# The second feed-forward stage of a transformer kernel, from plain products to block products with seven multiplications

## The reference, cut to what matters

```
mix = jnp.concatenate([y_pool, y_sb], axis=-1) @ w_out[i]
h = h + rms_norm_2(mix, g_mix_post[i])

m = rms_norm_2(h, g_mlp_pre[i]) @ w_up[i]
m = jnp.square(jax.nn.relu(m)) @ w_down[i]
h = h + rms_norm_2(m, g_mlp_post[i])
```

## Time and profile before

| | |
|---|---|
| median of 3 runs | 2649.5 us (2647.52 to 2650.82) |
| profiled execution, its own time | 2642.97 us |
| its span, first to last instruction | 2641.2 us |
| PE busy | 2422.6 us, 92% of the span |
| DVE / ACT / POOL busy | 1435.7 / 897.7 / 1034.2 us |
| mean granted TensorE clock | 0.952 of full speed |
| second feed-forward at full pace | from 1819.02 us on, to 2493.71 us |

### The profile page before, as it was taken

One profiled execution on the slowest core, in us unless ns is written; L12 is line 12 of the kernel. 1 busy time (PEld: TensorE's weight loads), 2 busy tenths in 40 slices (PEclk: granted clock), 3 DMA queues, 4 the chain that ended last, 5 costly groups with the idle time before them and its releaser, 6 DMA issues.

```text
span 2641.2 us, 28134 instructions
## 1 busy us (share of the span) xinstructions
PE 2422.6 (92%) x10656; PEld 1886.1 (71%) x10656; DVE 1435.7 (54%) x1534; ACT 897.7 (34%) x1339; POOL 1034.2 (39%) x628
## 2 busy tenths in 40 slices
PE   8988877989999999999788887968999999999978
PEld 6855645868888878877555554656888888888757
DVE  7788863586656666477355456457222222222566
ACT  4255554244444432221365466213001100110231
POOL 1000000468878778774111020244333334444353
PEclk9999988989999999999899896989999999999989
DMA  3211101314344368832000000211111111111102
GB/s 126 56 33 30 32 17 64 120 41 151 128 175 160 136 257 323 343 140 80 16 25 16 9 8 1 104 40 32 48 48 48 48 48 48 48 48 48 56 32 88
DMA packets 64540, 215.86 MB, mean 82 GB/s; under 512 B 20465, under 2 KB 20465, under 8 KB 57905
## 3 DMA queue, kind: packets, MB, share of 16 engines
q1 hardware_dynamic: 63776, 210.03, 22.1%
q10 hardware_dynamic: 656, 4.41, 0.4%
HBM read 161.24 MB, written 53.35 MB: 81 GB/s over the span
## 4 chain that ended last, share of the span: by engine, by line
PE 69%; issue 11%; DVE 10%; ACT 5%; POOL 4%; DMA 1%; SPq 0%; POOLq 0%; DVEq 0%; ACTq 0%
PE ps L702 39%; PE ps L971 21%; PE ps L1173 3%; DVE conv_out L1915 1%; PE ps L1105 1%; POOL weight_hi L578 1%; POOL weight_lo L580 1%; ACT sb_e L1694 1%; DMA weight_raw<-w_out 1%; ACT sb_e L1692 1%; POOL turn_weights L616 1%; POOL branch_out L661 1%; ACT sb_e L1696 1%; DVE sb_softplus_lo L2437 1%; PE ps L1148 1%
## 5 line engine op out<-in xcount | busy, mean ns | idle before, releaser
L578 POOL TENSOR_TENSOR weight_hi<-weight_raw,zero_col 128x1024 fp32r<-128x1024 f32 (+1 forms) x106 | 205.2, 1936 | 1371.7 <-PE ps L702 1111.0
L971 PE MATMUL ps<-operand,turn_weights 128*128 128x512 f32 x1848 | 427.0, 393 | 11.9 <-DVE operand L2112 7.2
L702 PE MATMUL ps<-input_lo,weight_hi 128*128 128x512 f32 x1328 | 419.2, 397 | 16.7 <-DVE gate_lo L2548 14.9
L702 PE MATMUL ps<-input_hi,weight_hi 128*128 128x512 f32 x1200 | 387.2, 404 | 50.5 <-DVE input_lo L1873 32.1
L971 PEld LDWEIGHTS ps<-operand,turn_weights 128*128 128x128 f32 x1848 | 350.2, 190 | 89.0 <-issue 13.6
L702 PE MATMUL ps<-input_hi,weight_lo 128*128 128x512 f32 x1200 | 374.5, 394 | 0.0
L702 PEld LDWEIGHTS ps<-input_lo,weight_hi 128*128 128x128 f32 x1328 | 254.5, 192 | 74.3 <-ACT input_lo L1279 11.4
L702 PEld LDWEIGHTS ps<-input_hi,weight_hi 128*128 128x128 f32 x1200 | 224.5, 192 | 112.0 <-issue 52.9
L616 POOL TENSOR_TENSOR turn_weights<-turn_raw,turn_weights 128x512 fp32r<-128x512 f32 (+1 forms) x170 | 234.5, 1390 | 93.7 <-ACT turn_weights L1279 92.8
L580 POOL TENSOR_TENSOR weight_lo<-weight_raw,weight_hi 128x1024 fp32r<-128x1024 f32 (+1 forms) x106 | 262.7, 2478 | 8.3
L702 PEld LDWEIGHTS ps<-input_hi,weight_lo 128*128 128x128 f32 x1200 | 228.5, 190 | 48.9
(11 more groups left out here) (299 smaller groups left out, 3689.4 us busy)
## 6 DMA issues: line engine op xcount, KB each, us to landing
hidden_operand<-hidden_kept SPq DMA_DIRECT2D x35, 1024.0 KB, 8.5
hidden_kept<-hidden_parts SPq DMA_DIRECT2D x22, 1024.0 KB, 11.2
turn_raw<-w_ff SPq DMA_DIRECT2D x40, 512.0 KB, 3.9
hidden_kept<-hidden_parts SPq DMA_DIRECT2D x11, 1536.0 KB, 8.9
weight_raw<-w_mlp SPq DMA_DIRECT2D x32, 512.0 KB, 3.3
weight_raw<-w_mlpd SPq DMA_DIRECT2D x32, 512.0 KB, 3.3
turn_raw<-w_ffd SPq DMA_DIRECT2D x20, 512.0 KB, 4.3
weight_raw<-w_out SPq DMA_DIRECT2D x16, 512.0 KB, 3.3
```

Of the source, the lines that this page charges most:

```text
L578: pool_.tensor_tensor(WH[:, slot, 0:width], raw, ZERO[:].to_broadcast([P, width]), ALU.add).then_inc(s["w_hi"], 1)
L702: last = mm(PS[:, b + 2 * c + h, :], w[:, slot, k * n + P * c:k * n + P * (c + 1)], a[:, k, h * H2:(h + 1) * H2], start=(k == first and st ...
L971: ins = mm(PS[:, b, :], weights(p, w, k), tokens(p, a, k), start=(FRESH[p] and k == 0 and step == 0), stop=(k == n - 1 and step == 2), ski ...
```

## The change

The second feed-forward gets the same treatment as the first: an instance `FF_B` with 16 hidden turns and 16 output turns. What differs from `FF_A`: there is no gate, so one turn makes a whole pair, and seven parts are made and written out in every turn, not in every second one. The blocks stay in PSUM: relu with scale (DVE) and square (ACT) work in place, and the sums of blocks go to PSUM too. Of seven products, three (p = 0, 1, 2) are copied by ACT (`kept_term`) to be added to later ones. The squares for the norm ahead of the stage are summed by TensorE (`add_to_mean`, a matmul with the mean matrix for each row) and no longer by DVE. POOL no longer scales rows; DVE does it.

```diff
+FF_B = Ff(1, FF_A.end, FF2 // P // 2, tuple((2 * g, 2) for g in range(NG2)), (0, 1, 2, 3, 4, 5, 6),
+          (32, 40, 48, 56, 64, 72, 80, 88, 128, 136), (0, 3, 5, 1, 4, 2, 6), 1)
...
@@ SP
+            turn_load(FF_B.t0)
+            turn_load(FF_B.t0 + 1)
+            for k in range(KD):
+                x_kept(FF_B, k)
+            stage_transfers(FF_B)
+            def stage_transfers(ff):
+                for t in range(ff.t0 + 2, ff.t2 + 2):
+                    turn_load(t)
...
+                    elif t >= ff.t0 + 3:
+                        parts_out(ff, t - 3 - ff.t0)
+                for p in range(N_PROD):
+                    parts_in(ff, 0, p)
...
@@ POOL
-            pool.wait_ge(s["scale_ready"], 4)
-            for k in range(1, KD):
-                pool_.tensor_tensor(MM[:, k, :], MM[:, k, :], RS[:], ALU.mult).then_inc(s["post_scaled"], 1)
-            splits(U_MLP + 2, U_PLEP - U_MLP - 2)
+            for t in range(FF_B.t0, FF_B.end):
+                turn_split(t)
...
@@ TensorE
+                if n == 0 and ff is FF_B:
+                    pe.wait_ge(s["scale_ready"], 4)
+                    for k in range(4):
+                        add_to_mean(k)
...
+                    elif ff is FF_B:
+                        if p in (0, 1, 3):
+                            pe.wait_ge(s["st_fl"], N_PROD * pairs_to(ff, n - 2))
...
+                    if p in (2, 4, 5):
+                        pe.wait_ge(s["st_mid"], 3 * (FF_A.n1 * ff.index + n) + {2: 1, 5: 2, 4: 3}[p])
                     elif p == 6:
                         pe.wait_ge(s["st_read"], read_at(t, 4))
...
-            with pe.Fori(1, NG2) as i:
-                ff_group(i, U_MLP, G, 1, 0)
+            for t in range(FF_B.t0, FF_B.t2):
+                hidden_turn(FF_B, t)
+            for t in range(FF_B.t2, FF_B.end):
+                output_turn(FF_B, t)
...
@@ ScalarE, one hidden turn
+                for q in range(3):
+                    block_hi(n - 1, q)
+                kept_term(t, 0)
+                turn_hi(t + 1, 0)
+                block_hi(n - 1, 3)
+                block_hi(n - 1, 4)
+                kept_term(t, 1)
+                turn_hi(t + 1, 1)
+                block_hi(n - 1, 5)
+                block_hi(n - 1, 6)
+                kept_term(t, 2)
+                turn_hi(t + 1, 2)
+                turn_hi(t + 1, 3)
+                squared(t, 0)
...
+            def block_hi(n, q):
+                act.wait_ge(s["st_sqd"], 6 * (n + 1))
+                act.wait_ge(s[f"st_sp{(0, 0, 0, 1, 1, 2, 2)[q]}"], 16 * pairs_to(FF_B, n - 1))
...
@@ VectorE, each row ahead of the stage
-                    dve.wait_ge(s["post_scaled"], k)
-                stt(X[:, k, :], MM[:, k, :], g("g_mix_post", k), X[:, k, :], ALU.mult, ALU.add)\
-                    .then_inc(s["post_x"], 1)
+                mark = chain(stt(MM[:, k, :], MM[:, k, :], g("g_mix_post", k), RS[:], ALU.mult, ALU.mult))
+                chain.wait(mark)
+                tt(X[:, k, :], X[:, k, :], MM[:, k, :], ALU.add).then_inc(s["post_x"], 1)
+                first_sums(FF_B, k, "g_mlp_pre")
+            other_operands(FF_B, "g_mlp_pre")
+            for j in range(4):
+                op_lo(FF_B, 6, j, raw_at(FF_B, 6, j))
             scale_from(5)
...
@@ VectorE, one hidden turn
+                total(3, 0, b0 + 1)
+                block(0, b0 + 1, lower)
+                total(4, 1, 6 + t % 2, "st_read")
+                dve.wait_ge(s["st_read"], read_at(t, 4))
+                block(1, 6 + t % 2, upper)
+                total(5, 2, b0 + 2)
+                block(2, b0 + 2, upper)
+                dve.wait_ge(s["st_prod"], prod(t, 6))
+                block(3, b0, lower)
...
+            for t in range(FF_B.t0, FF_B.t2):
+                if t > FF_B.t0:
+                    block_parts(t - FF_B.t0 - 1)
+                squared_terms(t)
```

More of the change, by code:

```diff
@@ L129, with __init__ @@
 class Ff:
-    def __init__(self, t0, n1, groups, place, ring):
-        self.t0, self.n1, self.groups, self.place, self.ring = t0, n1, groups, place, ring
+    def __init__(self, index, t0, n1, groups, place, ring, kept, reads):
+        self.index, self.t0, self.n1, self.groups, self.place, self.ring = index, t0, n1, groups, place, ring
+        self.kept, self.reads = kept, reads
         self.t2 = t0 + n1
@@ L1789, in _ @@
+            for t in range(FF_B.t2, FF_B.end - 1):
+                for p in range(N_PROD):
+                    turn_hi(t + 1, p)
+                    if t == FF_B.t2 + 2 and p > 3:
+                        last_hi(p - 4)
+                    elif t == FF_B.t2 + 3 and p < 4:
+                        last_hi(p + 3)
             act.wait_ge(s["ple_p_in"], 16)
@@ L2094, in _, with op_at, op_sum @@
             lower, upper = slice(0, H2), slice(H2, T)
[L2096 to L2099 removed]
+            def op_at(ff, p, part, j):
+                return FORM[ff.place[p]][:, part, j, :]
+            def op_sum(ff, p, j, out, x, gain, y, op):
                 if gain is None:
@@ L2265, in output_term @@
                 dve.wait_ge(s["st_read"], reads_to(t) + p)
-                last = p in (3, 4, 5, 6) and g_ == len(ff.groups) - 1
+                last = p in (3, 4, 5, 6) and g_ == len(ff.groups) - 1 and ff is FF_A
                 if g_ == 0 and p in (0, 1, 2, 6):
@@ new lines, in block_parts, with total, lo @@
+            def block_parts(n):
+                t = FF_B.t0 + n
+                b0, there, spare = 3 * (t % 2), PS[:, 6 + t % 2, :], PS[:, 7 - t % 2, :]
+                one, two, three = PS[:, b0 + 1, :], PS[:, b0 + 2, :], PS[:, b0, :]
+                done, low_ = 4 * (PAIRS_A + n), N_PROD * (PAIRS_A + n)
+                def total(i, out, x, y, op):
+                    tt(out, x, y, op).then_inc(s["st_ft"], 1)
+                    dve.wait_ge(s["st_ft"], done + i)
+                def lo(q, src):
+                    dve.wait_ge(s["st_fh"], low_ + q + 1)
+                    tt(STG[:, q, 1, :], src, STG[:, q, 0, :].bitcast(f32), ALU.subtract).then_inc(s["st_fl"], 1)
+                dve.wait_ge(s["st_sqd"], 6 * (n + 1))
+                if n:
+                    dve.wait_ge(s["st_fl"], low_)
+                total(1, spare, two, TB[:, lower], ALU.subtract)
+                total(2, two, TB[:, upper], two, ALU.subtract)
+                total(3, TA[:, upper], TB[:, upper], spare, ALU.subtract)
+                lo(0, one)
+                lo(1, three)
+                dve.wait_ge(s["st_fl"], low_ + 2)
+                total(4, three, three, TA[:, upper], ALU.subtract)
+                lo(2, there)
+                lo(3, spare)
+                lo(4, two)
+                lo(5, TA[:, upper])
+                lo(6, three)
@@ new lines, in _ @@
+            for t in range(FF_B.t0, FF_B.t2):
+                if t > FF_B.t0:
+                    block_parts(t - FF_B.t0 - 1)
+                squared_terms(t)
+            for t in range(FF_B.t2, FF_B.end):
+                for p in range(N_PROD):
+                    output_term(FF_B, t, p)
+                    if FF_B.group(t)[0] == 1:
+                        last_pair_of(FF_B, t, p)
+                    elif t == FF_B.end - 1 and p < 2:
+                        dve.wait_ge(s["ple_hi"], p + 1)
+                        tt(PPL[:, p, :], PPF[:, p, :], PPH[:, p, :].bitcast(f32), ALU.subtract)\
@@ L2532, in p_and_squares @@
                             .then_inc(s["ple_lo"], 1)
+                    elif t == FF_B.end - 1 and p < 6:
+                        add_square()
+            for k in range(4, KD):
                 add_square()
-                if m:
-                    add_square()
-            dve.wait_ge(s["bank_free"], (NG2 - 1) * (2 * G) + U_MLP)
-            dve.wait_ge(s["ff_acc"], (NG2 - 1) * 4)
-            ff_lo(NG2 - 1, U_MLP, G, 1, h0, MM, beside=p_and_squares)
-            add_square()
             scale_from(6)
+            dve.wait_ge(s["st_back"], 16 * 4)
```

610 lines of the change are left out of this document (330 added, 280 removed).

## The result

The changed kernel took 2604.0 us (median of four runs, 2598.8 to 2606.9), beside 2648.5 us for the kernel before, also of four runs (2646.0 to 2650.8): a ratio of 0.983, 95% interval 0.981 to 0.985, which is 44.5 us less. The forecast was 2603.5 us. The profiled execution took 2602.29 us with a span of 2600.5 us.

A forecast was written before the change was run, and what follows sets the result against it. Bound: TensorE's matmuls, and the seams between them. Stage end 2493.7 to 2445.1, 48.6 us less, 2.5 more at the tail: 46 less, 2597 profiled; plus 6.5 for the median, 2603.5 us, range 2592 to 2621.

The forecast's parts named there:

- The matmuls: Second feed-forward: 2688 matmuls instead of 3072 at 0.2268 us, 87.1 us less; hidden turns of 19.05 us, nothing charged.
- The seam ahead: Before the second feed-forward: DVE's instruction list is the bound, so product 6 of the first turn starts at 1847.7 us.
- (a): Last sum of squares ahead of the stage: 1.9 us less, scale ready at 1769.0 us instead of 1770.87.
- Rows: Seam ahead: DVE's work on the eight residual rows takes 49.7 us, the last row done at 1818.7 us.
- (c): Seam ahead: 24 DVE operations for the other tiles, 16.6 us uncontended; ACT's guess sets the middle, ending at 22.7 us.
- The restart: TensorE starting again at half clock at product 6 of the first turn: 1.6 us more until it is back up.
- The seam to the output turns: From hidden to output turns: the first operand's read follows the last writes, 1.5 us, bounds 0 and 3 us.
- The tail: Behind the stage, up to the mean: squares and adds one by one, and DVE running late, 2.5 us more.
- The stretched turns: Hidden turns: the 1.7 us to spare at product 2 used up, 1 us a turn, 16 us, 2619 us; chance 0.13.
- starved output turns: Output turns that also read the residual back: DMA too slow, up to 5 us, 2609 us; chance 0.07.
- The slower case: Hidden turns: high parts wait for the last pair's landing in the single buffer; 23 us a turn, 2663 us; chance 0.05.
- the fourth rival: DMA starving output turns: 17 MB in two turns, 43 us of 38 at 410 GB/s, up to 5 us; chance 0.07.

The follow-up runs named there:

- blocks_sbuf: Changed kernel with the squared blocks of every hidden turn written to SBUF, not PSUM; 2605.9 us, ratio 0.9851 to before.
- rows_ahead: Changed kernel with DVE adding residual row k+1 before it makes the operands of row k; 2590.6 us, ratio 0.9783 to before.
- guess_late: Changed kernel with ACT's first guess of the scale moved behind the high parts of operands 4 and 5; 2601.8 us.
- read_early_copy: read_early, with ACT's copy of the second turn's first kept term moved right behind the second block's squares; 2596.2 us.
- seam_read_first: Changed kernel with the output turns' first operand read issued ahead of the writes of the last but one pair's parts; 2597.4 us.
- parts_twice: Changed kernel with each portion of parts written to device memory twice, the next pair's high parts waiting for both writes; 2630.4 us.
- tail_even_first: Changed kernel with ACT squaring rows 4, 6, 5, 7 after the last output term, the first two one term earlier; 2594.2 us.
- together_late_read: Changed kernel with the edits of rows_ahead, guess_late, seam_read_first and tail_even_first; 2582.4 us, ratio 0.9748 to before.
- read_early: Changed kernel with the first turn's two sums that need no scale taken ahead of operand 6's low parts and the scale; 2603.4 us.

## Why the prediction was right, point by point

**The matmuls.** Predicted 2688 at 0.2268 us, a hidden turn of 19.05 us, nothing charged for the 16 turns. The 240 us window without a pause shows it, and blocks_sbuf shows why it was safe: 2.5 us more on DVE and 1.5 us more on POOL in each turn cost nothing there. The latency was counted well too: in the third turn ACT's copy of product 0 ended at 1879.24 us and product 2 was due at 1881.1, 1.8 us to spare where 1.7 was predicted. The 1050 ns that the prediction took for an operation with both sides in SBUF is a mean of fast and slow ones (shortest, median and longest in ns):

```profile
L2235 DVE TENSOR_TENSOR hidden_parts<-hidden_parts x26: 678/840/1777, 650.7 to 880.4; 128x512 fp32r<-128x512 f32 x26
```

**The seam ahead.** From the mean to the first row 7.59 us (before 7.83); the last sum of squares 1.86 us in place of 3.09, so (a) gave 1.2 + 0.2 us and not 1.9: POOL, which was to stand still from about 1760 us, worked until 1763.8, into this sum. Rows: 49.9 us, predicted 49.7. The 24 operations and the rest to product 6: 28.4 us, predicted 29.0. That this list bounds the seam is shown by rows_ahead, us for us. A reason within (c) was wrong, and the time came out right all the same: ACT's guess does not set it (guess_late), and by the durations it is POOL beside DVE's operations that makes it 22 us and not 16.6.

**The restart.** Predicted 1.6 us. From product 6 to the first output product 293.25 us passed, of which 1272 matmuls are 288.5 and the gap 1.89: 2.9 us at half clock (granted 0.50 from 1851 to 1857 us). The term was mis-sized, since it counted half clock only "until it is back up" from a few matmul pairs of the earlier trace rows; nor is it one number: it was 2.0 us in rows_ahead and guess_late, and in read_early_copy the clock was at 1.00 from product 6 on.

**The seam to the output turns.** Predicted 1.5 us, plus 1.0 for small waits in the output turns. Measured 1.89 and 0.1. The mechanism, the read behind the last writes, is shown by seam_read_first, and parts_twice moves it the other way.

**The stage.** From the mean ahead of it to its end: 730.7 us before, 683.9 after, 46.8 us less; the forecast's 48.6 less the 1.9 ahead of the mean is 46.7.

**The tail.** Predicted 2.5 us more. From the stage's end to the span's end it is 151.5 us in place of 147.5, 4.1 more: the mean comes 2.0 us later, and the next unit starts 1.2 us later behind it, at a granted clock of 0.54 after a wait of 2.96 us, where it was 1.00 after 0.94 us. This second part was not in the sum. It is no fixed price of the change, since two kernels with the same wait did not pay it. tail_even_first took 1.9 of the 2.0 us back. The remaining 0.9 us I did not trace; kernels with the same tail differ by as much as 1.1 us there.

**The total.** The profiled executions differ by 40.7 us, the medians by 44.5, and 46 was forecast. The forecast for the profiled execution was 2597 us, and it took 2602.3, 5.3 us more: the mean ahead of the stage started 2.0 us later than before where 1.9 us earlier was forecast, and the tail was 1.6 us longer than forecast. The late start lies inside the 8.5 us by which equal code scatters there, so no single execution can say whether the change has a part in it. The other way, 6.5 us were added for the distance of the median from the profiled execution, and for the changed kernel that distance was 1.7. The two misses cancel: the hit to half a microsecond is luck. The terms of the stage and of the tail were within 2 us each.

**The rivals.** The stretched turns and the starved output turns did not occur. The slower case was rightly placed but priced too steeply: with twice the writing a turn took 20.26 us, by the rate, not 23. In the fourth rival 17 MB at 410 GB/s are 41.5 us and not 43, which changes nothing. A figure of the Trainium skill stood against my sum (DMA: Bandwidth & Descriptors, Specifications, about 358 GB/s between device memory and one core): windows of the changed kernel show 386 GB/s with PE full, of together_late_read 410, and of parts_twice 425, so here the measurement decides.

## What to carry to other kernels

When a stage becomes pure matmuls at full clock, count the matmuls first, then write out the list of the engine that bounds each seam instruction by instruction; here 13.7 us taken from DVE's list were worth 14.1 us, and moving ACT's guess out of the way of the same seam nothing. Before you free a product earlier, look at what the next ones wait for: product 6 came 8.5 us earlier and 4.4 us of that went into two waits for ACT's copies one turn later. Slack in the middle of a stage hides slower work, but the same lateness comes out at its end, where the last result is waited for. And before you explain 1 to 4 us by an edit, compare the granted clock behind each wait, also where the edit changes nothing.

## What the runs showed of the hardware that was not expected

- DVE and POOL slow each other down when both of DVE's inputs are in SBUF: DVE from 0.69 us to between 1.67 and 1.78 us, POOL from 1.30 to 1.73 us (128x512, fp32). With one input in PSUM DVE stays at 0.70. In the turn of blocks_sbuf shown above the one that began first, by 0.07 us, kept its time and the other paid.
- The same wait of TensorE ended at either clock: after 2.96 us ahead of the mean behind the stage the granted clock was 0.50 to 0.54 in most kernels and 1.00 in two, and at the first output product it was 0.58 after 1.84 us (read_early) and 1.00 after 1.87 us (read_early_copy).
- One core moved 416 GB/s between SBUF and device memory from 1880 to 2120 us of parts_twice, 425 in one window of 40 us, reading weights and writing parts together.
- Code ahead of the change, the same in the changed kernel and the ten built on it, was done at times 8.5 us apart in the profiled executions.
